# Attention by single heads and 1024 queries, or by head pairs and 512 queries with the sums of p on TensorE

## What is computed

```python
def one_block(qi):
    s = jnp.einsum('bqhgd,bkhd->bhgqk', qi, k, preferred_element_type=F32) * scale
    p = jax.nn.softmax(s, axis=-1).astype(v.dtype)
    return jnp.einsum('bhgqk,bkhv->bqhgv', p, v)
```

## Time and profile before

| | us |
|---|---|
| median of 3 runs | 4966.51 |
| lowest, highest | 4954.9, 4967.96 |
| span of the profiled execution | 4960.5 |

### The profile page before, as it was taken

One profiled execution on the slowest core, in us unless ns is written; L12 is line 12 of the kernel. 1 busy time (PEld: TensorE's weight loads), 2 busy tenths in 40 slices (PEclk: granted clock), 3 DMA queues, 4 the chain that ended last, 5 costly groups with the idle time before them and its releaser, 6 DMA issues. The chain is left out here.

```text
span 4960.5 us, 50531 instructions
## 1 busy us (share of the span) xinstructions
PE 4101.6 (83%) x20550; PEld 2205.4 (44%) x20550; DVE 2666.5 (54%) x4012; ACT 1456.2 (29%) x1904; POOL 727.9 (15%) x394
## 2 busy tenths in 40 slices
PE   6795449699897979999998596368799986999996
PEld 5453338233333555555554454356233432444443
DVE  2773666577786063323334683655699954333334
ACT  1322233244453232111112221333355533212121
POOL 0001221044444000000000000310255530000000
PEclk7897665687897969999999797655699988999998
DMA  4210012100000221111110210021000020211110
GB/s 160 52 30 1 1 62 85 35 9 8 5 1 20 91 64 43 43 39 39 43 39 32 54 38 1 1 96 66 21 10 4 1 68 0 73 47 56 47 51 34
DMA packets 207642, 194.46 MB, mean 39 GB/s; under 512 B 9719, under 2 KB 174386, under 8 KB 206770
## 3 DMA queue, kind: packets, MB, share of 16 engines
q1 hardware_dynamic: 203250, 182.84, 11.8%
q10 hardware_dynamic: 4160, 8.39, 0.4%
HBM read 167.48 MB, written 14.68 MB: 37 GB/s over the span
## 5 line engine op out<-in xcount | busy, mean ns | idle before, releaser
L324 PE MATMUL mlp_acc<-hh,mlp_w 128*128 128x512 f16 (+1 forms) x3840 | 753.2, 359 | 52.4 <-DVE mlp_w L314 52.4
L324 PE MATMUL mlp_acc<-mlp_aa,mlp_w 128*128 128x512 f16 (+1 forms) x3840 | 749.2, 358 | 0.0
L324 PEld LDWEIGHTS mlp_acc<-hh,mlp_w 128*128 128x128 f16 x3840 | 376.5, 98 | 427.1 <-DVE mlp_w L314 53.3
L324 PEld LDWEIGHTS mlp_acc<-mlp_aa,mlp_w 128*128 128x128 f16 x3840 | 375.8, 98 | 371.1
L1393 POOL TENSOR_TENSOR at_acc<-at_acc,at_p 128x1024 f32<-128x1024 f32 x192 | 482.7, 2514 | 354.5 <-ACT at_p L1429 350.7
L1496 DVE TENSOR_TENSOR at_plo<-at_p,at_phi 128x1024 f16<-128x1024 f32 (+1 forms) x264 | 461.1, 1755 | 63.9 <-ACT at_phi L1432 56.9
L324 PE MATMUL in_acc<-hh,in_w 128*128 128x512 f16 (+1 forms) x2088 | 400.5, 355 | 71.5 <-DVE in_w L314 59.0
L1429 ACT ACTIVATE at_p<-at_sT 128x1024 f32<-128x1024 f32 (+1 forms) x264 | 254.9, 966 | 504.1 <-PE at_sT L1575 498.9
L1451 DVE TENSOR_REDUCE at_mx<-at_small 128x1 f32<-128x512 f32 (+1 forms) x600 | 326.5, 585 | 117.4 <-PE at_small L1524 116.0
L666 DVE SCALAR_TENSOR_TENSOR yf<-mlp_acc,yf 128x1280 f32<-128x1280 f32 (+1 forms) x112 | 151.9, 1357 | 398.7 <-PE mlp_acc L324 398.7
L653 DVE TENSOR_TENSOR mlp_r<-mlp_r 128x1280 f32<-128x1280 f32 (+1 forms) x64 | 86.9, 1358 | 476.8 <-ACT mlp_r L634 476.8
(11 more groups left out here) (272 smaller groups left out, 5584.1 us busy)
## 6 DMA issues: line engine op xcount, KB each, us to landing
mlp_stage<-in_w_ff SPq DMA_DIRECT2D x128, 512.0 KB, 3.8
pa_wada<-in_w_ada SPq DMA_DIRECT2D x16, 2048.0 KB, 8.0
in_stage<-in_w_in SPq DMA_DIRECT2D x36, 512.0 KB, 4.2
set_wada<-in_w_ada ACTq DMA_DIRECT2D x4, 2048.0 KB, 19.7
out_stage<-in_w_out SPq DMA_DIRECT2D x16, 512.0 KB, 4.9
nf_wada<-in_w_ada SPq DMA_DIRECT2D x4, 2048.0 KB, 8.1
x<-x_scratch SPq DMA_DIRECT2D x1, 5120.0 KB, 16.9
xin<-in_x SPq DMA_DIRECT2D x8, 512.0 KB, 6.0
```

Of the source, the lines that this page charges most:

```text
L324: last = self.nc.tensor.matmul(acc[0:mw, a:a + c], w[:, wh, k, m0:m0 + mw], src[:, sh, k0 + k, a:a + c], start=(k == 0 and wh == 0 and sh ...
```

## The change

The whole of `attention` is written anew around **head pairs**. A unit is now two heads and 512 latent queries (ten steps), twelve in each layer; in layer 0 a short unit of two heads and 256 context queries (two steps) follows every second one. A step still has 128 keys and 1024 (head, query) columns, now as 2 x 512.

- `weighted` runs three steps behind (`LAG`). It writes two accumulators in PSUM, the weighted values and the sums of p, for both heads at once: head 0 of the pair to partitions 0 to 63, head 1 to partitions 64 to 127. It has ten matmuls of 64 weight columns: high values x `phi`, low values x `phi`, high values x `plo`, a block of ones x `phi`, the block x `plo`, each for the two heads in turn. All 64 partitions of a head hold the same sum, so nothing has to be spread.
- `plo` is computed by VectorE in all steps (`on_dve`), GpSimd's additions and the `sum` and `cast` tasks are gone; GpSimd sets the block of ones.
- Behind a unit ScalarE copies both accumulators (`copy_sums`), and VectorE takes the reciprocal of 128 x 512 sums, multiplies and splits (`finish`).
- The `max` tasks of the next unit are spread evenly over steps 0 to 7: 24 of them three a step, 28 (with a short unit) four in steps 0 to 3 and three in steps 4 to 7. They alternate between the heads of the pair, and in group A read the queries where they lie (partitions 0 to 63 and 64 to 127) instead of the placed copy. VectorE takes them behind the step's `plo`.
- `p32` and `plo` have four buffers, `phi` five, in place of three each; queries are placed by pair, two deep.

```diff
-LEAD = 2
+LAG = 3
 EARLY = 2
+PRING, HRING, LRING = 4, 5, 4
...
-    for h in range(12):
-        units.append((h, 0, LAT, list(range(TT))))
-        if l < DEPTH - 1:
-            units.append((h, LAT, CTX, [TT - 2, TT - 1]))
+    for pr in range(6):
+        units += [(pr, 0, 512, list(range(TT))), (pr, 512, 512, list(range(TT)))]
+        if full:
+            units.append((pr, LAT, CTX, [TT - 2, TT - 1]))
...
+    long = [u for u in range(U) if units[u][2] == 512]
+    on_dve = [True for u, s in steps]
...
+    def maxes(u):
+        pr, q0, n, kts = units[u]
+        return [("max", u, par, q, c) for q in range(n // P) for c in range(len(chunks(len(kts) * P))) for par in range(2)]
+
...
+        for t in maxes(0):
+            put((-1, 0), t)
+        for par in range(2):
+            put((-1, 0), ("row", 0, par))
+        for k, u in enumerate(long):
+            nxt = list(range(u + 1, long[k + 1] + 1)) if k + 1 < len(long) else list(range(u + 1, U))
+            todo = [t for v in nxt for t in maxes(v)]
+            for s in range(8):
+                take = -(-len(todo) // (8 - s))
+                for t in todo[:take]:
+                    put((u, s), t)
+                todo = todo[take:]
+            for v in nxt:
+                for par in range(2):
+                    put((u, 9), ("row", v, par))
...
+        p32 = sb("p32", [P, PRING, 2, 512])
+        phi, plo = sb("phi", [P, HRING, 2, 512], F16), sb("plo", [P, LRING, 2, 512], F16)
+        mx, neg = sb("mx", [P, U, 2, 4, 3]), sb("neg", [P, U, 2, 4])
+        po, rc, o32 = sb("po", [P, 2, 2, 512]), sb("rc", [P, 512]), sb("o32", [P, 512])
+        ones = sb("ones16", [P, 64], F16)
+        sT = [ps(f"sT{i}", [P, 2, 512]) for i in range(2)]
+        acc = ps("acc", [P, 2, 512])
...
+                    if pr >= 2:
+                        sp.wait_ge(s_S, base[units.index((pr - 1, 0, 512, list(range(TT))))])
...
+                        for a, n, qhi, qlo in spread(f.aq[64 * par:64 * par + 64, pr, :], nq):
+                            place(qq[0:64, pr % 2, par, :], a, n, qhi, s_load[pr % 2])
+                            place(qq[64:P, pr % 2, par, :], a, n, qlo, s_load[pr % 2])
+                            place(qs[0:64, pr % 2, par, :], a, n, qhi, s_load[pr % 2])
...
+                    pool.wait_ge(s_e16, i + 1)
+                    if i >= LRING:
+                        pool.wait_ge(s_pv, i - LRING + 1)
+                    nc.gpsimd.tensor_tensor(plo[:, i % LRING, :, 0:n], p32[:, i % PRING, :, 0:n],
+                                            phi[:, i % HRING, :, 0:n], ALU.subtract).then_inc(s_plo, 1)
...
+                def copy_sums(u):
                     n = units[u][2]
                     act.wait_ge(s_pv, base[u + 1])
-                    if u:
-                        act.wait_ge(s_ov, u)
...
+                        act.wait_ge(s_read, u - 1)
+                    nc.scalar.activation(po[:, u % 2, :, 0:n], acc[:, :, 0:n], ACT.Copy).then_inc(s_po, 1)
...
+                    nc.scalar.activation(p32[:, i % PRING, :, 0:n], sT[i % 2][:, :, 0:n], ACT.Exp).then_inc(s_e32, 1)
+                    if i >= HRING:
+                        act.wait_ge(s_pv, i - HRING + 1)
+                    nc.scalar.activation(phi[:, i % HRING, :, 0:n], sT[i % 2][:, :, 0:n], ACT.Exp).then_inc(s_e16, 1)
+                    rows((u, s))
+                    while done < U and base[done + 1] - 1 <= i - LAG:
+                        copy_sums(done)
+                        done += 1
...
+                    dve.wait_ge(s_po, u + 1)
...
+                    ch(nc.vector.reciprocal(rc[:, 0:n], po[:, u % 2, 1, 0:n]))
...
+                    nc.vector.tensor_tensor(o32[:, 0:n], po[:, u % 2, 0, 0:n], rc[:, 0:n], ALU.mult).then_inc(s_read, 1)
+                    dve.wait_ge(s_read, u + 1)
+                    ch(nc.vector.tensor_copy(hi, o32[:, 0:n]))
+                    ch.wait(dve)
+                    ch(nc.vector.tensor_tensor(lo, o32[:, 0:n], hi, ALU.subtract))
...
                 for i, (u, s) in enumerate(steps):
                     n = units[u][2]
-                    small_tasks((u, s), ("max",))
...
+                    if on_dve[i]:
+                        dve.wait_ge(s_e16, i + 1)
+                        if i >= LRING:
+                            dve.wait_ge(s_pv, i - LRING + 1)
+                        nc.vector.tensor_tensor(plo[:, i % LRING, :, 0:n], p32[:, i % PRING, :, 0:n],
+                                                phi[:, i % HRING, :, 0:n], ALU.subtract).then_inc(s_dlo, 1)
+                    maxima((u, s))
+                    while done < U and base[done + 1] - 1 <= i - LAG - 1:
+                        finish(done)
...
-                def small_tasks(where, part=slice(None)):
+                def tasks(where, part=slice(None)):
...
                         if j >= 2:
-                            released(pe, j - 2)
-                        out = small[j % 2]
+                            pe.wait_ge({"max": s_max, "row": s_row}[kinds[j - 2]], nth(kinds[j - 2], j - 2))
...
+                            if pr < 4:
+                                R = slice(64 * par, 64 * par + 64)
+                                last = nc.tensor.matmul(out[:, 0:w], hi_of(f.aq[R, pr, :], q0 + q * P),
+                                                        kk[R, pr // 2, a:a + w], start=True, stop=True)
...
+                def scores(i):
+                    u, s = steps[i]
+                    pr, q0, n, kts = units[u]
+                    if s == 0:
+                        pe.wait_ge(s_row, rows_through[u])
+                    if i >= 2:
+                        pe.wait_ge(s_e16, i - 1)
+                    K = slice(kts[s] * P, (kts[s] + 1) * P)
+                    for par in range(2):
+                        pairs = score_pairs(pr, par)
+                        for j, (k, q) in enumerate(pairs):
+                            last = nc.tensor.matmul(sT[i % 2][:, par, 0:n], k[:, K], q[:, q0:q0 + n],
+                                                    start=(j == 0), stop=(j == len(pairs) - 1))
+                    last.then_inc(s_S, 1)
...
                 def weighted(i):
...
                     if s == 0 and u:
-                        pe.wait_ge(s_ov, u)
...
+                    def part(bank, j, of, p):
+
+                        for par in range(2):
+                            v = value(pr, par, kts[s])
+                            w = {"hi": v[:, 0:64], "lo": v[:, 64:P], "one": ones[:, :]}[of]
+                            ins = nc.tensor.matmul(acc[64 * par:64 * par + 64, bank, 0:n], w, p[:, par, 0:n],
+                                                   start=(s == 0 and j == 0),
+                                                   stop=(s == len(kts) - 1 and j == (2, 1)[bank]), skip_group_check=True)
+                        return ins
+
+                    part(0, 0, "hi", phi[:, i % HRING])
+                    part(0, 1, "lo", phi[:, i % HRING])
+                    part(0, 2, "hi", plo[:, i % LRING])
+                    part(1, 0, "one", phi[:, i % HRING])
+                    part(1, 1, "one", plo[:, i % LRING]).then_inc(s_pv, 1)
...
+                    scores(i)
+                    tasks((u, s), slice(0, EARLY))
+                    if i >= LAG:
+                        weighted(i - LAG)
+                    tasks((u, s), slice(EARLY, None))
+                for i in range(N - LAG, N):
+                    weighted(i)
```

More of the change, by code:

```diff
@@ L1262, in attention @@
[L1262 to L1289, removed]
-    tasks_ = [tasks[j] for w in order for j in at[w]]
-    n0 = 0
-    for w in order:
-        at[w] = list(range(n0, n0 + len(at[w])))
-        n0 += len(at[w])
-    tasks = tasks_
-    kinds = [t[0] for t in tasks]
@@ L1297, in attention, with put @@
-    nth = lambda kind, i: kinds[:i + 1].count(kind)
     steps = [(u, s) for u in range(U) for s in range(len(units[u][3]))]
+    N = len(steps)
     base = {u: sum(len(units[v][3]) for v in range(u)) for u in range(U + 1)}
+    long = [u for u in range(U) if units[u][2] == 512]
+    on_dve = [True for u, s in steps]
+    lows_dve = [sum(on_dve[:i + 1]) for i in range(N)]
+    lows_pool = [i + 1 - lows_dve[i] for i in range(N)]
+    small, at = [], {}
+    def put(where, task):
+        at.setdefault(where, []).append(len(small))
+        small.append(task)
@@ L1300, in attention @@
+    plan()
+    kinds = [t[0] for t in small]
+    nth = lambda kind, j: kinds[:j + 1].count(kind)
     with ExitStack() as st:
@@ L1415, in read_pv @@
-                def read_pv(u):
+                        if small[j][0] != "row":
+                            continue
+                        _, u, par = small[j]
+                        pr, q0, n, _ = units[u]
+                        row, R = shift_row(pr, par)
+                        act.wait_ge(s_small, j + 1)
+                        nc.scalar.activation(row[:, q0:q0 + n], sm[j % 2][R:R + 1, 0:n], ACT.Copy).then_inc(s_row, 1)
+                def copy_sums(u):
```

(14 more changed lines are left out.)

305 lines of the change are left out of this document (99 added, 206 removed).

## The result

The changed kernel takes **5222.6 us** (median of 4 runs, 5215.7 to 5233.4) against 4967.2 for the kernel before, measured beside it: a ratio of 1.051 [1.049, 1.054]. Forecast 5345, range 5120 to 5500. The profiled execution has a span of 5231.6 us.

A forecast was written before the change was run, and what follows sets the result against it. A loop through four engines, closed once a step by maxima taken behind `plo`, was to bound the changed kernel. 4966.5 us + 191 (attention at the upper clock level) + 188 (lower clock) gave 5345 us, range 5120 to 5500.

The forecast's parts named there:

- The loop: Attention steps with maxima: scores, both exps, `plo`, reading a maximum, next maximum matmul, next scores; 5.25 us, heads 8 to 11 5.69.
- rival 1: Attention steps: the loop doesn't close and the engines' sums of work decide; about 4790 us, chance 0.08.
- A unit at the upper level: Ten attention steps at the higher TensorE clock: 52.0 us for heads 0 to 7, 56.4 for heads 8 to 11.
- The steps behind the maxima: Steps 8 and 9 of a unit, without maxima: 2.4 us, then 4.4 at the boundary to the next unit.
- the division: `finish` of each unit on VectorE: 5.3 us of work, of which 3.2 us fall on the loop.
- under 4 in steps 8 and 9: Sign that the forecast is right: in layer 1, steps 8 and 9 take under 4 us from step to step.
- Layers: Attention at the upper level: layer 1 622 us (+119), layer 0 673 us (+75), prologues -3; +191 us in all.
- `plo` and `finish`: VectorE's work: `plo` 1.23 us beside an idle GpSimd; in `finish` a reciprocal of 3.35 and a cast of 0.55 us.
- `weighted`: Five matmul pairs a step on TensorE, the two column halves side by side: 1.1 us at the upper level, off the path.
- Rival 2: Column halves do not overlap in f16, so `weighted` streams 2.2 us and the clock mostly stays up; 5265 us, chance 0.10.
- The 0.11 us a matmul: Possible extra cost of each `weighted` matmul without the fast weight load: 1.1 us a step, not moving the sum.
- the clock, +188 us: TensorE at its lower level for 0.6 of the time: 13.6 us more a unit, 23 units; bounds 0 and 313.
- Rival 3: The clock stays at the lower level whenever the loop binds; 5470 us, chance 0.12.

The follow-up runs named there:

- Number 1: Changed kernel with VectorE taking a step's maxima ahead of that step's `plo`, as the kernel before did: 4806.5 us, ratio 0.966.
- number 10: Changed kernel with nine of the ten `weighted` matmuls in one column half, output wrong: 5202.2 us, ratio 1.047.
- number 5: Changed kernel with five more pairs of matmuls on zero weights a step, filling TensorE's standstill: 5213.7 us, ratio 1.049.
- number 8: Changed kernel with maxima ahead of `plo` and `weighted` issued head by head instead of alternating column halves: 4850.5 us, ratio 0.975.
- number 12: Changed kernel with maxima ahead of `plo` and nine of the ten `weighted` matmuls in one column half: 4975.5 us, ratio 1.000.
- number 2: Changed kernel with `weighted` issued head by head instead of alternating column halves: 5183.8 us, ratio 1.041.
- number 4: Kernel before the change, with its maxima moved behind the step's `plo`: 5595.6 us, ratio 1.124.
- number 7: Changed kernel with maxima ahead of `plo` and the division cut into four blocks behind `plo` of steps 8 and 9: 4763.4 us, ratio 0.958.

## Why the prediction was right, and where its sizes were off

- **The loop.** Forecast 5.25 us; measured 5.25 and 5.15 by turns, 5.58 and 5.48 for heads 8 to 11 (5.69), and 6.32 and 6.10 at the lower level (6.34). TensorE waits 2.0 us for a maximum, as forecast, in 115 waits in layer 1 (88 put down). Number 1 takes the loop away by order alone and gives 4806, where rival 1 (the loop doesn't close) had been put at 4790: both ends of that argument held, though the step is not an even 3.5 us there but 2.8, with one of 8.9 a unit.
- **A unit at the upper level.** Forecast 52.0 and 56.4; measured 52.1 and 55.5. The steps behind the maxima were 2.18 and 4.17 (2.4 and 4.4), the division added 8.88 - 5.2 = 3.7 (3.2). The sign "under 4 in steps 8 and 9" failed for step 9 and contradicted the forecast's own 4.4.
- **Layers.** Less the clock's 90 us, attention grew by 256 - 90 = 166 us against +191. Layer 1 is 657 - 36 = 621 (622). The 25 us are in the prologues (-8, not -3) and in layer 0: 110.0 a pair (112.0), heads 8 and 9 115.7 (120.8), and the last pair some 8 us shorter.
- **`plo` and `finish`.** 1.225 us with GpSimd idle (1.23), reciprocal 3.344, cast 0.426 (0.55 taken).
- **`weighted`.** Pairs side by side in f16, as taken from the f32 rows; at the upper level four take 0.62 us, and the next pairs start 0.22 apart:

```profile
3713.43 0.62 PE L1534 MATMUL at_acc<-at_phi,av 128*64 128x512 f16 x4
3713.88 0.38 PE L1534 MATMUL at_acc<-at_plo,av 128*64 128x512 f16 x2
3714.10 0.38 PE L1534 MATMUL at_acc<-at_phi,at_ones 128*64 128x512 f16 x2
3714.31 0.38 PE L1534 MATMUL at_acc<-at_plo,at_ones 128*64 128x512 f16 x2
```

  Rival 2's mechanism is out, yet number 10, which builds it, shows its reasoning was half right: without overlap the clock was 0.89 and 0.90. It came to 5202, not 5265. By the Trainium skill's TensorEngine Tiling (Array Packing), Feature Incompatibilities, column tiling excludes the fast weight load. The 0.11 us a matmul that I had weighed beside that, from the earlier trace rows, doesn't show here: the pairs keep to 0.22 (0.43 at the lower level).
- **The step that was mis-sized: the clock, +188 us, measured some 90.** Its share was nearly right: granted clocks of 0.72 and 0.74 are 0.56 and 0.52 of the time at the lower level, against 0.6, which had been judged and not worked out, so that hit is partly luck. Its price was not right. I had let steps 8 and 9 cost 5.8 us more at the lower level (12.6 for 6.8, with no working for the 12.6). But TensorE can be back at 2.4 GHz in the boundary (the pairs 0.22 us apart above stand right behind one), and ScalarE, whose times don't change, sets much of it: step 8 took 4.09 instead of 2.18, step 9 4.17 in both, so 1.9 us. And the step with the division is shorter, not longer, where the step ahead of it was at the lower level (8.03 against 8.88). A unit at the lower level thus costs some 7 x 1.0 + 1.9 - 0.85 = 8.1 us, not 13.6; with the share, 23 x 8.1 x 0.54 = 100 us, near the 90 of number 5. With 90 for 188 and 166 for 191, the forecast of 5345 becomes 5222; that the two add up is no test, since 166 is what 256 leaves over 90, and the split is good to some 10 us. Both terms were put too high, so no error hid another.
- **Rival 3** (the clock stays down, 5470) fails on both: the share is 0.54, and even at 1 its price would be about 23 x 8.1 = 186, not 313.

## What to carry to other kernels

Draw the order of each engine's queue as a graph and look for a cycle through one step: with two small buffers and three small tasks a step, an in-order engine that puts the long work ahead of the short reads serialises everything, however much busy time the change saves. Then ask of each part of a change separately: here a 5% loss was a 5% gain with two lines in the other order and one condition changed. And when you price a lower clock, add it only to the parts of the chain that are TensorE's own work, and ask what else sets the rest.

## What the runs showed of the hardware that was not expected

- Matmuls issued five by five to the two column halves did not run one after the other: ten took 1.35 us, the second half's starts 0.03 us behind the first's (number 8). With nine of ten in one half they did run one after the other (number 12: `weighted` 2.0 us).
- At the same step of 5.2 us, the less time TensorE's matmuls filled, the lower the granted clock was: 0.72 and 0.74 with pairs side by side, 0.82 and 0.85 with the heads one behind the other (number 2), 0.89 and 0.90 with nine of ten in one half, 0.92 and 0.93 with five pairs on zero weights added.
- `plo` of 1.23 us became 2.38 in the mean beside GpSimd's addition of 2.41, which started 0.87 us ahead of it in the step shown (number 4).
- A reciprocal of 128 columns with its three followers and their hand-overs takes 1.96 us, so four of them take 7.8 where one of 512 takes 5.3 (number 7).
